# A two-block transformer kernel: 144 unread products in place of five, in front of the norm that feeds the retention

## What is computed

```python
def first_block(...):
    ...
        h = h + 0.5 * g2 * _swiglu(_prenorm(h, norm_ffn2[layer], sh2, sc2), ffn2_w_in[layer], ffn2_w_out[layer])
    ...
    return _rmsnorm(h, final_norm)

def second_block(x, ...):
    for i in range(DEPTH):
        if i % N_MIXERS == 0:
            mix = retention(x, ret_w_in[j], ret_w_out[j])
        ...

def _rmsnorm(x, g):
    xf = x.astype(jnp.float32)
    y = xf * lax.rsqrt(jnp.mean(xf * xf, axis=-1, keepdims=True) + NORM_EPS)
    return (y * g.astype(jnp.float32)).astype(x.dtype)
```

## Time and profile before

| | |
|---|---|
| median of 2 runs | 2644.22 us (2640.85 and 2647.59) |
| the profiled execution, its own time | 2638.45 us |
| its span, first to last instruction | 2636.7 us |
| PE busy | 2586.2 us, 98% of the span |
| PEld, DVE, ACT, POOL busy | 87%, 56%, 40%, 8% |
| mean granted TensorE clock | 0.994 |
| chain that ended last | PE 89%, DVE 4%, issue 3%, ACT 2%, DMA 1% |

### The profile page before, as it was taken

How to read it: one execution, slowest core, us unless ns; L and a number is a source line. 1 busy time by engine, 2 the same in 40 slices (tenths; PEclk the granted TensorE clock), 3 DMA queues, 4 the chain that set the end, 5 groups by cost and what they waited for, 6 DMA issues and landing times.

```text
span 2636.7 us, 40528 instructions
## 1 busy us (share of the span) xinstructions
PE 2586.2 (98%) x17486; PEld 2283.1 (87%) x17486; DVE 1483.3 (56%) x1987; ACT 1042.5 (40%) x1406; POOL 198.4 (8%) x192
## 2 busy tenths in 40 slices
PE   8999999999999999999999999999999999999998
PEld 6788888877888888888888899999999999988998
DVE  5666654746556546553345575565555554565655
ACT  4221223634222224212233554453754454555544
POOL 0000000211000000000011000010020020144001
PEclk9999999999999999999999999999999999999999
DMA  8444445114435445442153165565445566763462
GB/s 279 160 164 162 152 157 173 49 62 161 151 126 167 137 136 178 142 159 97 60 185 112 49 202 187 183 211 167 144 159 194 179 194 187 218 148 120 151 208 90
DMA packets 376081, 405.99 MB, mean 154 GB/s; under 512 B 7264, under 2 KB 352176, under 8 KB 375904
## 3 DMA queue, kind: packets, MB, share of 16 engines
q1 hardware_dynamic: 375904, 403.40, 47.5%
HBM read 402.25 MB, written 1.12 MB: 153 GB/s over the span
## 4 chain that ended last, share of the span: by engine, by line
PE 89%; DVE 4%; issue 3%; ACT 2%; DMA 1%; POOL 0%; SPq 0%; POOLq 0%; DVEq 0%; ACTq 0%
PE bank L98 88%; DVE w_lo L109 1%; PE bank L101 1%; ACT w_hi L105 1%; POOL acc L109 0%; DMA w_raw<-in_ffn_w_in 0%; DMA w_raw<-in_ada_w 0%; SPq L135 0%; ACT x_hi L105 0%; DVE tmp L117 0%; DVE df_sc L126 0%; ACT df_e L106 0%; DVE hT L117 0%; ACT at_pT L105 0%; DVE hT L109 0%
## 5 line engine op out<-in xcount | busy, mean ns | idle before, releaser
L109 DVE TENSOR_TENSOR w_lo<-w_raw,w_hi 128x2048 fp32r<-128x2048 f32 (+3 forms) x333 | 698.7, 2102 | 740.0 <-ACT w_hi L105 739.3
L98 PE MATMUL bank<-x_hi,w_hi 128*128 128x256 f32 (+1 forms) x3000 | 976.5, 326 | 4.4 <-DVE w_lo L109 2.5
L98 PE MATMUL bank<-x_hi,w_lo 128*128 128x256 f32 (+1 forms) x3000 | 967.0, 323 | 0.0
L98 PE MATMUL bank<-x_lo,w_hi 128*128 128x256 f32 (+1 forms) x3000 | 962.5, 323 | 0.0
L105 ACT ACTIVATE w_hi<-w_raw 128x2048 fp32r<-128x2048 f32 (+3 forms) x333 | 579.2, 1743 | 385.1 <-PE bank L98 223.4
L98 PEld LDWEIGHTS bank<-x_hi,w_hi 128*128 128x128 f32 x3000 | 564.3, 188 | 64.1 <-issue 13.6
L98 PEld LDWEIGHTS bank<-x_hi,w_lo 128*128 128x128 f32 x3000 | 564.1, 188 | 47.6
L98 PEld LDWEIGHTS bank<-x_lo,w_hi 128*128 128x128 f32 x3000 | 562.4, 188 | 47.1 <-issue 0.7
L98 PE MATMUL bank<-hid_hi,w_hi 128*128 128x512 f32 (+1 forms) x1056 | 353.2, 335 | 0.0
L98 PE MATMUL bank<-hid_hi,w_lo 128*128 128x512 f32 (+1 forms) x1056 | 351.6, 333 | 0.0
L98 PE MATMUL bank<-hid_lo,w_hi 128*128 128x512 f32 (+1 forms) x1056 | 351.4, 333 | 0.0
(11 more groups left out here) (281 smaller groups left out, 2340.9 us busy)
## 6 DMA issues: line engine op xcount, KB each, us to landing
w_raw<-in_ffn_w_in SPq DMA_DIRECT2D x88, 1024.0 KB, 6.1
w_raw<-in_ada_w SPq DMA_DIRECT2D x72, 1024.0 KB, 8.3
w_raw<-in_ffn_w_up SPq DMA_DIRECT2D x44, 1024.0 KB, 5.2
w_raw<-in_attn_w_in SPq DMA_DIRECT2D x36, 1024.0 KB, 5.4
w_raw<-in_ffn_w_out SPq DMA_DIRECT2D x32, 768.0 KB, 5.1
w_raw<-in_ret_w_in SPq DMA_DIRECT2D x24, 1024.0 KB, 5.5
w_raw<-in_ffn_w_out SPq DMA_DIRECT2D x32, 640.0 KB, 4.1
w_raw<-in_odd_w_in SPq DMA_DIRECT2D x12, 1024.0 KB, 5.3
```

The lines of the kernel that those rows point to most:

```text
L98: return Issued(self.eng and self.eng.matmul(out, lhsT, rhs, start=start, stop=stop, skip_group_check=loose))
L109: return Issued(self.eng and self.eng.tensor_tensor(out, a, b, op))
```

## The change

In `pe_rms_rows`, where the norm is not one of those with a modulation step (the norm in front of the retention alone), the five products of constants are replaced by `pe_series`. It issues twelve series of twelve products, 144 in all, on the contents of `x2.hi` (stationary) and `x2.lo` (moving), into the spare bank. In each series the twelve products are the same one; the series differ in the number of columns (512, 256 or 128) and in the order in which the moving operand's columns are read. The four products of constants behind the statistics and the five behind the rows stay. Nothing else is altered.

```diff
+def turned(ap, a):
+    return ap.rearrange("p (a b) -> p b a", a=a)
+
+
+def pe_series(e):
+
+    k = e.k
+    bank = e.bank("spare", None, None)
+    del e.used[k.bank_at["spare"]]
+    hi, lo = (t[:, 0:4, :].rearrange("p a b -> p (a b)") for t in (k.x2.hi, k.x2.lo))
+    all, some = bank[:, 0:2 * T], bank[:, 0:T]
+    two, one, far = lo[:, 0:2 * T], lo[:, 0:T], lo.rearrange("p (a b) -> p a b", a=4)
+    still = hi[:, 0:P]
+    series = [(all, still, two),
+              (all, still, turned(two, 2)),
+              (all, still, two.rearrange("p (a b c) -> p b a c", a=2, c=2)),
+              (all, still, two.rearrange("p (a b c) -> p b a c", a=2, c=16)),
+              (all, still, far[:, 0:4:2, :].rearrange("p a b -> p b a")),
+              (some, still, one),
+              (some, still, turned(one, 2)),
+              (some, still, far[:, 0:2, 0:P].rearrange("p a b -> p b a")),
+              (some, hi[:, T:T + P], far[:, 2:4, 0:P].rearrange("p a b -> p b a")),
+              (some, still, one.rearrange("p (a b c) -> p b a c", a=2, c=16)),
+              (bank[:, 0:T // 2], still, lo[:, 0:P]),
+              (some, hi[:, 0:2 * P].rearrange("p (b a) -> p a b", a=2)[:, 0, :], turned(one, 2))]
+    for out, lhsT, rhs in series:
+        for _ in range(12):
+            e.matmul(out, lhsT, rhs, True, True)
+
+
@@ pe_rms_rows @@
     if nid in NORM_STEPS:
         pe_ada_one(e)
     else:
-        pe_keep_busy(e, 5)
+        pe_series(e)
     e.wait_ge(k.pooled, ("sum", nid, KC - 2))
```

## The result

| | before | after |
|---|---|---|
| median of 2 executions each, lowest to highest | 2644.22 us (2640.85 to 2647.59) | 2667.48 us (2661.47 to 2673.50) |
| ratio, 95% interval | | 1.0105 (1.0081 to 1.0129) |
| span of the profiled execution | 2636.7 us | 2671.7 us |
| first replaced product to `ones,acc` | 1.82 us | 24.55 us |

What stands behind the number is another matter: one term of the sum, the extra price of jumping columns, was wrong by 11 us and in sign, and the number came out near by luck. One execution among the experiments, of the version in "The order put to use", took 2881.96 us at a mean granted clock of 0.847 and is left out of its median.

What follows compares the result with a forecast made beforehand. PE was taken to bound the kernel, busy 98% of the span. Added products of 33.9 us (23.0 at contiguous price plus 10.9 for jumping columns) less 2.27 us hidden gave +31.6 us on 2640.85: 2672.5 us, range 2657 to 2688 us.

Steps and rivals of the forecast that it cites:

- the extra price of jumping columns: In six of the added series, columns read by jumps cost twice the contiguous price, 0.885 ns each, adding 10.9 us.
- the cover: At the replaced constants, the wait for POOL's sum hides 1.82 us and the table load 0.45 us, 2.27 us in all.
- S - 2.27 us: The norm and all behind it come later by the added products' time, 33.9 us, less 2.27 us hidden: +31.6 us.
- Contiguous columns: Added products cost 0.226 us at 512 columns, 0.113 at 256, 0.11 at 128; 23.0 us if every order costs the same.
- the bound below it: For jumping columns in the added series: at least the contiguous 0.442 ns a column, since a worse order cannot be quicker.
- Runs of two and sixteen at the contiguous price: Series 3, 4 and 10 left at the contiguous price; doubling series 3 would add 2.7 us.
- The doubled load of 0.22 us: In series 12, taking every second stationary column could double the load from 0.11 us, hidden by its doubled stream of 0.226 us.
- The Trainium skill: Its 16-byte line rule, two accesses for full bandwidth, makes series 2, 5, 7, 8, 9 and 12 pay, not 3; no size.
- The chip's clock and what follows: Around the norm the granted clock stays full (1.00), and nothing in the chain behind pays the delay back.
- Case A: In the added series order is free, 0.442 ns a column anywhere: +20.7 us, 2661.6 us; chance 0.27.
- Rival B: In the added series jumping columns collide at power-of-two distances, 3.2 ns a column: +88 us, 2729 us; chance 0.07.
- C: At the added series, loads or products are saved or run beside the down-projection: at most +0 us, 2640.9 us; chance 0.02.

Runs made afterwards that it cites:

- The order put to use: Kernel before, no added series, feed-forward operands stored with even tokens in one half of a row and odd in the other: 2587.15 us against 2645.10, ratio 0.9786.
- the first experiment: Changed kernel with all twelve series and the last one's stationary operand in contiguous order: 23.60 us from first product to `ones,acc`, 0.95 us less than the changed kernel.

## Why the prediction was right, and where it was not

- **What bounds the kernel, and the cover.** Right. S - 2.27 us was the formula; with the measured 24.55 us it gives 22.28 us, and the place costs 22.20 us. POOL's sum and the table load are covered as foreseen, and the square root follows the product after 0.04 us.
- **Contiguous columns.** Right for the price: 13.6 us for sixty was 0.226 us each, measured 0.227. The 256-column ones came at 0.118 to 0.120 and not 0.113 us, 0.07 us more for series 6. The 0.11 us for 128 columns held (1.29 us for 1.3).
- **Jumping columns: the step that failed.** "I take twice the contiguous price, 0.885 ns", and the bound below it, "a worse order cannot be quicker". Measured 216 / 512 = 0.422 ns a column, 5% under the contiguous price. Series 2, 5, 7, 8, 9 and 12 took 10.7 us where 21.8 stood in the sum; read contiguously (the first experiment) they take 11.25 us, so that the term of +10.9 us was in truth -0.6 us. The bound was wrong because it took contiguous for the best order without a row that says so. The price itself leaned on the earlier trace rows, and those rows were misread. The program's first products stream contiguous columns and have nothing to say on order. What they show fits a change of clock: their starts are 427 ns apart up to 13.03 us and 235 and 230 ns from 13.34 us on, and the trace's first record of a granted clock, at full, begins at 13.18 us. In the trace of the changed kernel the step from 427 to 236 ns comes at its own first record, 11.10 us, and in its repetition at 10.50 us. Before that record the views print 1.00 without having one. That 427 ns is the lower of TensorE's two clocks (512 columns at 1.2 GHz are 427 ns) fits these numbers; no record of the granted clock covers the stretch.
- **Runs of two and sixteen at the contiguous price.** Wrong the other way: series 3 took 4.07 for 2.7 us, series 4 2.89. All that the sum had outside the six jumping series was 12.1 us, and it took 13.9.
- **The stationary operand of series 12.** The doubled load of 0.22 us does not appear: the products come every 0.121 us. But neither is it free, as series 7 with the same moving operand has 0.112 us.
- **The Trainium skill** was weighed here: the note on SBUF "cachelines" in "SBUF — State Buffer". The lines of 16 bytes are there (250 against 330 to 340 ns by the start of the run). The condition of at least two accesses to a line, one behind the other, is not what the runs show. One column in turn from two places never has two and costs least; pairs always have two and cost half as much again; every second column has two to a line and costs double. Where the penalty is largest, it is about a doubling (443 to 487 ns for 227): steps within one place, pairs from four places, eight places in turn.
- **The chip's clock and what follows.** Right for the clock: 1.00 in every stage of the series. Right that nothing is paid back (15.97 us from the square root to PE's restart, before 15.96).
- **The number.** 2672.5 us was forecast and 2667.48 us measured. By the place alone it should have been 2640.85 + 22.2 = 2663 us; the profiled one of the changed kernel's two executions, 2673.50 us, had the slow rate in four of the five long runs behind the place. With more executions the median was 2660.99 us. So the forecast came within 5 us of the measured median by luck: the series were priced 9 us too dear, and the median of two executions lay 4 us above what the place costs. Case A, which had 0.27 (2661.6 us), described the time better than the case that was forecast, though for a reason that is not true either: the order is not free, it is 5 to 7% cheaper in five of the series and up to 50% dearer in others.
- **Rival B** fell: the distance, a power of two or not, plays no part (216 ns at 258 elements too). **C** fell: all 144 products are in the trace, one behind the other, and PEld's instructions rose by the same 134 as PE's (17486 to 17620, ten of the constants gone).

## What to carry to other kernels

Where products bound a kernel, the order in which the moving operand lies in SBUF is worth a probe: here two interleaved halves took about 57 us off 2644 with as many products as before (17486 instructions on PE in both), and in the probes a step of two within a row doubled the time of a product. The stationary operand wants its own probe. A probe of a dozen equal products in an otherwise unchanged kernel, read by the distance between starts, measures such a thing to a nanosecond, where whole executions scatter by 10 us. And a bound for something that the trace does not show needs a reason for its sign: "cannot be quicker" was an assumption. Nor does a row carry over because it is slow: look for what made it slow first.

## What the runs showed of the hardware that was not expected

- Moving columns of fp32r are served as if by two readers, one for the even and one for the odd places of the order, each fetching lines of four columns (16 bytes). Spacing of 512-column products: a new line for each reader in four of its columns 216 ns, in two 227 ns, in one 451 ns. The model fits most series within 5%, and misses runs of four to thirty-two columns by 4 to 10% and eight places in turn by 8%; that there are two readers in the hardware is not shown.
- Contiguous order is not the quickest: 227 ns against 216 ns.
- A stationary operand that takes every second column raises the spacing of 256-column products from 112 to 121 ns (series 7 and 12).
- A run of contiguous 256-column products keeps one of two rates, 113.3 or 117.8 ns, at the same granted clock. The rate of the same run differed between two executions of one program, and changed between two runs of one execution though PE did not pause.
- The first products of the program come every 427 ns until the trace's first record of a granted clock, and every 227 to 236 ns behind it (at 13.18, 11.10 and 10.50 us in three executions).
- ACT and DVE pay 1.8 and 1.6 times for writing one element in turn into two halves (1121 and 1116 ns for 632 and 692; DVE reads one of its inputs in that order too), and 1.4 and 1.2 times for reading every second element and writing contiguously (858 and 838 ns).
